# Six of eight attention-gate tiles in Strassen units ahead of attention, and a reordered start of the attention stage

## The reference

```
h = x + 0.5 * SwiGLU_1(RMSNorm(x))
u = RMSNorm(h)
[xp | q | k | v | gate_logits] = u @ w_in      # 512 | 512 | 512 | 512 | 2048 columns
y_pool = (causal multi-scale pooling of xp) @ w_branch_pool
y_sb   = (strictly causal stick-breaking attention, 8 heads of 64) @ w_branch_attn
m = sigmoid(g_pool) * y_pool + sigmoid(g_sb) * y_sb
h = h + m @ w_out
h = h + 0.5 * SwiGLU_2(RMSNorm(h))
out = RMSNorm_final(h)
```

## Time and profile before

| what | value |
|---|---|
| median of 3 runs | 1917.43 us (1917.35 to 1917.62) |
| the profiled execution, its own time | 1918.11 us |
| its span, first to last instruction | 1916.2 us |
| TensorE busy | 1903.5 us (99% of the span) |
| VectorE, ScalarE, GpSimd busy | 1372.2, 796.4, 115.9 us |
| granted TensorE clock, mean | 0.999 of full speed |
| mix stage, from its first to its last matmul | 707.7 to 821.9 us |
| attention stage | 909.3 to 1149.8 us |

### The profile page before, as it was taken

The page is one execution under the profiler, slowest core; times in us unless marked ns, Lnnn a source line. Parts: engine busy times, 40 slices in busy tenths (PEclk is TensorE's granted clock), DMA queues, the critical chain, the costliest instruction groups (busy, mean ns, idle before and its releaser), DMA issues.

```text
span 1916.2 us, 24977 instructions
## 1 busy us (share of the span) xinstructions
PE 1903.5 (99%) x9010; PEld 1592.0 (83%) x9010; DVE 1372.2 (72%) x1677; ACT 796.4 (42%) x1175; POOL 115.9 (6%) x157
## 2 busy tenths in 40 slices
PE   9999999999999999999999999999999999999998
PEld 8888888888888888888888888898888888888887
DVE  6978777784566776488677768889777777756555
ACT  7423232323434544234676752474323232324344
POOL 1000000000000300000233220010000000000001
PEclk9999999999999999999999999999999999999999
DMA  5456654558676733416875447643545444677665
GB/s 165 144 198 230 223 181 140 199 189 306 208 240 201 195 110 132 132 50 181 226 174 148 128 139 260 197 138 119 178 144 196 149 169 153 216 264 244 206 192 206
DMA packets 258419, 348.24 MB, mean 182 GB/s; under 512 B 29344, under 2 KB 161184, under 8 KB 255008
## 3 DMA queue, kind: packets, MB, share of 16 engines
q1 hardware_dynamic: 258336, 347.15, 56.3%
HBM read 233.83 MB, written 112.99 MB: 181 GB/s over the span
## 4 chain that ended last, share of the span: by engine, by line
PE 97%; DVE 1%; DMA 1%; issue 0%; SPq 0%; ACT 0%; POOL 0%; POOLq 0%; DVEq 0%; ACTq 0%
PE bank L1263 40%; PE bank L1372 9%; PE bank L1319 9%; PE bank L1321 9%; PE bank L1320 9%; PE bank L1513 6%; PE bank L1215 3%; PE bank L1449 2%; PE bank L1421 2%; PE bank L1479 2%; PE bank L1585 2%; PE bank L1604 1%; PE bank L1190 1%; PE bank L1603 1%; PE bank L1570 1%; PE bank L1568 1%
## 5 line engine op out<-in xcount | busy, mean ns | idle before, releaser
L2253 DVE TENSOR_TENSOR dn_lo<-dn_lo_raw,dn_hi 128x1024 fp32r<-128x1024 f32 x149 | 181.9, 1224 | 149.6 <-ACT dn_hi L1788 149.1
L1263 PE MATMUL bank<-lo_t,wa_hi 128*128 128x512 f32 x656 | 252.8, 389 | 0.0
L1263 PE MATMUL bank<-hi_t,wa_hi 128*128 128x512 f32 x656 | 252.8, 389 | 0.0
L1263 PE MATMUL bank<-hi_t,wa_lo 128*128 128x512 f32 x656 | 252.8, 389 | 0.0
L1788 ACT ACTIVATE dn_hi<-dn_lo_raw 128x1024 fp32r<-128x1024 f32 x149 | 158.0, 1061 | 218.8 <-DMA dn_lo_raw<-act_dram 218.8
L1319 PE MATMUL bank<-dn_hi 128*128 128x512 f32 x596 | 232.7, 390 | 0.0
L1321 PE MATMUL bank<-dn_lo,dn_hi 128*128 128x512 f32 x596 | 231.9, 389 | 0.0
L1320 PE MATMUL bank<-dn_hi,dn_lo 128*128 128x512 f32 x596 | 231.9, 389 | 0.0
L1263 PE MATMUL bank<-hi_b,wa_hi 128*128 128x512 f32 x492 | 190.6, 389 | 1.0 <-DVE up L2387 1.0
L1263 PE MATMUL bank<-lo_b,wa_hi 128*128 128x512 f32 x492 | 190.5, 389 | 0.0
L1263 PE MATMUL bank<-hi_b,wa_lo 128*128 128x512 f32 x492 | 190.4, 389 | 0.0
(11 more groups left out here) (275 smaller groups left out, 3747.7 us busy)
## 6 DMA issues: line engine op xcount, KB each, us to landing
wa_lo_raw<-in_ffn_w_gate_up_dram SPq DMA_DIRECT2D x87, 512.0 KB, 5.0
dn_lo_raw<-act_dram SPq DMA_DIRECT2D x149, 256.0 KB, 4.2
act_dram<-g SPq DMA_DIRECT2D x44, 512.0 KB, 4.4
wd_t<-in_ffn_w_down_dram SPq DMA_DIRECT2D x44, 512.0 KB, 6.6
act_dram<-s_of SPq DMA_DIRECT2D x88, 256.0 KB, 6.5
wd_dram<-wd_t SPq DMA_DIRECT2D x22, 1024.0 KB, 6.0
dn_lo_raw<-wd_dram SPq DMA_DIRECT2D x85, 256.0 KB, 3.4
dn_lo_raw<-in_ffn_w_down_dram SPq DMA_DIRECT2D x64, 256.0 KB, 3.0
```

Source lines behind the costliest of these rows:

```text
L1263: last = nc.tensor.matmul(acc, lhs, rhs, start=n == 0 and i != 2 and i < 5, stop=n == 11, skip_group_check=True)
L2253: return nc.vector.tensor_tensor(dst, raw, hi.bitcast(f32), ALU.subtract)
```

## The change

Six gate tiles of kind 1 go through the mix stage in place of four: `EARLY` becomes 6, the mix stage has 7 units, the attention stage 5 gate units (480 matmuls), three of them of kind 0 alone. Since the number of units is now odd, the second plain q, k unit computes in banks 4 to 7 and the bank halves of the mix units are `(b + NM + 1) % 2`; the branch weights after attention swap their two buffers. `pool_y` gets a place of its own, and SP loads the first head and two blocks of `pool_y` ahead of the weights of gate unit 1. The four split pieces of that unit come later (`piece_step`). `SHARE` stays as it is.

```diff
-EARLY = 4
+EARLY = 6
...
-    return gate_step(piece_start(j) + (7 + 18 * piece if j < NG - 1 else 1 + 6 * piece))
+    return gate_step(piece_start(j) + (26 if j == 1 else 7) + (16 if j == 1 else 18) * piece if j < NG - 1 else piece_start(j) + 1 + 6 * piece)
...
-        pool_y = at("pool_y", [P, 2, HALF], f32, G0)
+        pool_y = at("pool_y", [P, 2, HALF], f32, o + 16384)
...
             gate_unit(0)
             spill_pool_branch(2)
-            gate_unit(1)
...
             load_head(0)
+            sp_.wait_ge(y_even_sp, 16)
+            load_pool_y(0)
+            sp_.wait_ge(y_sp[1], 16)
+            load_pool_y(1)
+            gate_unit(1)
             spill_pool_branch(3)
             load_head(1)
             for b in range(4):
                 sp_.wait_ge(y_sp[b], 16 * (KT // 2 if b else KT // 4))
             sp_.wait_ge(y_even_sp, 16 * (KT // 4))
-            load_pool_y(0)
-            load_pool_y(1)
             gate_unit(2)
...
-                    wait_bank(b, q)
+                    if not fresh:
+                        pe.wait_ge(tr_free, 4 * NT)
...
-                        last = products(bank[:, b, :], par, ab, lambda kt: u_hi[:, kt, cols],
+                        last = products(bank[:, b if fresh else 4 + b, :], par, ab, lambda kt: u_hi[:, kt, cols],
...
-                s = (b + 1) % 2
+                s = (b + NM + 1) % 2
...
-                    if b == 0 and i == 0:
-                        pe.wait_ge(tr_free, 4 * NT)
-                    if b == 1 and i in (0, 1, 3, 4):
-                        wait_bank(place, Q_A[1] + 1)
+                    if b < 2 and i in (0, 1, 3, 4):
+                        wait_bank(place, Q_A[b] + 1)
...
-                branch_tile(j, j % 2, j // 2)
+                branch_tile(j, (U_C + j) % 2, j // 2)
```

More of the change, by code:

```diff
@@ L1945, in take_first @@
                 act.wait_ge(acc_ready, 4 * Q_A[m] + b + 1)
-                nc.scalar.activation(ring_hi[n % 3][:, th * HALF:(th + 1) * HALF], bank[:, b, :], ACT.Copy,
+                nc.scalar.activation(ring_hi[n % 3][:, th * HALF:(th + 1) * HALF], bank[:, 4 * m + b, :], ACT.Copy,
                                      scale=1.0 if ab else QSCALE).then_inc(ev_hi, 1)
@@ L1969, in mix_first @@
                 act.wait_ge(mb_prod, 7 * b + 1)
-                nc.scalar.activation(mix_dst(b, 0, 0), bank[:, 4 * ((b + 1) % 2), :], ACT.Copy).then_inc(mb_copied, 1)
+                nc.scalar.activation(mix_dst(b, 0, 0), bank[:, 4 * ((b + NM + 1) % 2), :], ACT.Copy).then_inc(mb_copied, 1)
             def mix_second(b):
@@ L1976, in mix_second @@
                     act.wait_ge(mb_add, 5 * b)
-                nc.scalar.activation(mid[:, :], bank[:, 4 * ((b + 1) % 2), :], ACT.Copy).then_inc(mb_copied, 1)
+                nc.scalar.activation(mid[:, :], bank[:, 4 * ((b + NM + 1) % 2), :], ACT.Copy).then_inc(mb_copied, 1)
             def mix_post(b, a, th, adds):
@@ L2221, in outputs_hi @@
                 nc.scalar.activation(o_piece(u_hi, i), o_piece(xu, i), ACT.Copy).then_inc(o_hi, 1)
-            act.wait_ge(raw_in[KT % 2], 32 * (U_C // 2 + 1))
+            act.wait_ge(raw_in[U_C % 2], 32 * (U_C // 2 + 1))
             act.wait_ge(gate_ready, GATE_LAST[NG - 2] + 1)
-            nc.scalar.activation(w_hi[:, KT % 2, 0, 0:BR], w_raw[:, KT % 2, 0, 0:BR], ACT.Copy).then_inc(whi, 1)
+            nc.scalar.activation(w_hi[:, U_C % 2, 0, 0:BR], w_raw[:, U_C % 2, 0, 0:BR], ACT.Copy).then_inc(whi, 1)
             for i in range(len(O_PARTS)):
@@ L2232, in split_branch @@
             def split_branch(j):
-                act.wait_ge(raw_in[j % 2], 32 * ((U_C + j) // 2 + 1))
+                act.wait_ge(raw_in[(U_C + j) % 2], 32 * ((U_C + j) // 2 + 1))
                 act.wait_ge(acc_ready, 4 * Q_C + 2 * (j - 1))
-                nc.scalar.activation(w_hi[:, j % 2, 0, 0:BR], w_raw[:, j % 2, 0, 0:BR], ACT.Copy).then_inc(whi, 1)
+                nc.scalar.activation(w_hi[:, (U_C + j) % 2, 0, 0:BR], w_raw[:, (U_C + j) % 2, 0, 0:BR], ACT.Copy).then_inc(whi, 1)
             for n in range(1, KT):
@@ L2690, in take_first @@
                 cols = slice(th * HALF, (th + 1) * HALF)
-                nc.vector.scalar_tensor_tensor(out=ring_lo[(2 * m + ab) % 3][:, cols], in0=bank[:, b, :], scalar=1.0 if ab else QSCALE,
+                nc.vector.scalar_tensor_tensor(out=ring_lo[(2 * m + ab) % 3][:, cols], in0=bank[:, 4 * m + b, :], scalar=1.0 if ab else QSCALE,
                                                in1=ring_hi[(2 * m + ab) % 3][:, cols].bitcast(f32), op0=ALU.mult,
@@ L2755, in mix_c11 @@
                 dst = mix_dst(b, 0, 0)
-                nc.vector.tensor_tensor(dst, bank[:, 4 * ((b + 1) % 2) + 1, :], dst, ALU.add).then_inc(mb_add, 1)
+                nc.vector.tensor_tensor(dst, bank[:, 4 * ((b + NM + 1) % 2) + 1, :], dst, ALU.add).then_inc(mb_add, 1)
             def mix_c22(b, part):
-                dst, s = mix_dst(b, 1, 1), (b + 1) % 2
+                dst, s = mix_dst(b, 1, 1), (b + NM + 1) % 2
                 if part:
@@ L2776, in mix_c12 @@
                 dve.wait_ge(mb_prod, 7 * b + 6)
-                nc.vector.tensor_tensor(mix_dst(b, 0, 1), bank[:, 4 * ((b + 1) % 2) + 2, :], mid[:, :], ALU.add).then_inc(mb_add, 1)
+                nc.vector.tensor_tensor(mix_dst(b, 0, 1), bank[:, 4 * ((b + NM + 1) % 2) + 2, :], mid[:, :], ALU.add).then_inc(mb_add, 1)
             def mix_c21(b):
                 dve.wait_ge(mb_prod, 7 * b + 7)
-                nc.vector.tensor_tensor(mix_dst(b, 1, 0), bank[:, 4 * ((b + 1) % 2) + 3, :], mid[:, :], ALU.add).then_inc(mb_add, 1)
+                nc.vector.tensor_tensor(mix_dst(b, 1, 0), bank[:, 4 * ((b + NM + 1) % 2) + 3, :], mid[:, :], ALU.add).then_inc(mb_add, 1)
             def mix_out(b, a, th, posts):
@@ L3084, in _ @@
                     dve.wait_ge(whi, U_C + 1)
-                    nc.vector.tensor_tensor(flat(w_lo[:, KT % 2, 0, 0:BR]), flat(w_raw[:, KT % 2, 0, 0:BR]),
-                                            flat(w_hi[:, KT % 2, 0, 0:BR]).bitcast(f32), ALU.subtract).then_inc(wlo, 1)
+                    nc.vector.tensor_tensor(flat(w_lo[:, U_C % 2, 0, 0:BR]), flat(w_raw[:, U_C % 2, 0, 0:BR]),
+                                            flat(w_hi[:, U_C % 2, 0, 0:BR]).bitcast(f32), ALU.subtract).then_inc(wlo, 1)
             outputs_lo(len(O_PARTS) - 1)
@@ L3119, in split_branch @@
                 dve.wait_ge(whi, U_C + j + 1)
-                dst, raw, hi = (flat(w[:, j % 2, 0, 0:BR]) for w in (w_lo, w_raw, w_hi))
+                dst, raw, hi = (flat(w[:, (U_C + j) % 2, 0, 0:BR]) for w in (w_lo, w_raw, w_hi))
                 nc.vector.tensor_tensor(dst, raw, hi.bitcast(f32), ALU.subtract).then_inc(wlo, 1)
```

## The result

| | before | after |
|---|---|---|
| median of the runs | 1917.5 us (1917.35 to 1917.62, 4 runs) | 1932.0 us (1930.48 to 1933.13, 4 runs) |
| ratio, 95% interval | | 1.0074 (1.0062 to 1.0086) |
| profiled execution: own time, span | 1918.1, 1916.2 us | 1931.8, 1929.8 us |

The change makes the kernel 14.5 us slower. The forecast was 1918.9, its range ended at 1923.0: wrong in size, and the slower case had been given 0.27. One run of the kernel before, beside the first experiments, took 6375 us at a granted clock of 0.29 and is left out of every comparison.

A forecast was written before the change was run, and what follows sets the result against it. TensorE, busy 1903.5 of 1916.2 us, was taken as the bound, provided gaps between matmuls stay covered. Terms -2.7 - 0.8 + 5.0 = +1.5 us on the profiled execution gave 1918.9 us against the median, range 1914 to 1923.

The forecast's parts named there:

- Part 1: Mix and attention stages: one more mix unit adds 19.0 us, the gate unit it replaces frees 21.8; net -2.7 us.
- Part 3: Attention chain: fewer gate matmuls to cover it open 5.6 us of TensorE gaps; +5.0 us net, bounds 1.5 to 10.
- Weighings: TensorE gaps before the weighings of blocks (7,6), (5,4) and (3,2): 1.4, 0.4 and 1.9 us.
- Reserve 0.05: Block 6's transposes to the weighing of (7,6): 0.05 us to spare, one filler fewer, two in one head; 1.4 us.
- Transposes of block 5: Interval from block 0's transposes to block 5's: two fillers go against 0.34 us of reserve; 1.9 us of gaps in all.
- The -0.6 of relief: ScalarE in attention: four gate evictions and four weight pieces leave, some of them in a chain; -0.6 us.
- The GpSimd rival: GpSimd's products stretch attention scans in five named steps, four hits taken: 3.9 us on top, 1922.8 us; chance 0.23.
- Part 2: Start of attention: first head's keys load ahead of gate unit 1's weights, wait 1.8 to 1.0 us; -0.8 us.
- the megabyte is most of what stands ahead of those loads: Start of attention: gate unit 1's 1 MB of weights mainly delays the k_lo loads; reason for taking a 1.0 us wait.
- the other bound: Start of attention: keys land at 914.4 as before the change, wait 2.4 us, a loss of 0.6.
- the first loads only change places: Start of attention: the later spill holds up tile 2, keys gain nothing; +1.5 to +3 us, 1921; chance 0.05.
- The chain keeps up: Attention chain: gaps may not add, as one lengthens the next interval's start; 1 us in all, 1914.9 us; chance 0.27.

The follow-up runs named there:

- thinned: Kernel before with every sixth gate matmul of the attention stage left out, banks, products and pieces unmoved: 1909.8 us.
- the small products: Changed kernel with GpSimd's gate products cut to 8 of their 512 columns: 1926.6 us.
- the old order: Changed kernel with SyncE's old queue at the start of attention, gate unit 1's weights ahead of the first head, pool_y loads behind the second head's: 1930.0 us.
- the new places alone, with full cover: Changed kernel with 96 of its 480 attention-stage gate matmuls done twice, giving 576 as before: 1939.5 us.

## Why the prediction was wrong

**Part 1 held.** The mix stage is 19.0 us longer, gapless; the net of the matmuls is -2.7 us. The moved banks, ring places and branch buffers cost nothing that shows.

**Part 3 named the right mechanism and mis-sized it: 5.0 us forecast, 10.4 measured** in the chain of the kernel before with thinned fillers (13.5 - 3.1), and 14.1 in the changed kernel, where the new places come on top. Every interval that it listed opened. The errors, term by term, in the changed kernel:
- *Weighings.* The three terms, 3.7 us, measured 6.7. "Reserve 0.05" for (7,6) was no reserve: the changed kernel's gaps there are mostly 0.26 to 0.28, a whole filler over the 0.05 that already stood. The sum also left out the second filler that one head loses (0.2 us), and 0.8 us of the first head's gap is the late spill.
- *Transposes of block 5.* 1.9 against 5.4. I let this chain begin at block 0's transposes and counted two fillers. ScalarE is busy without a break from 974.62 until block 0's `at_hi` at 978.19: the backlog begins with block 5's own logits, whose sigmoids, the value split and an eviction stand in that queue. From those logits to the transposes stand 12 or 13 fillers in place of 15 or 16, so three or four went, up to 0.9 us per head. Moving the split (1.06 us) closed most of the gap in two of the three heads that prepare values. In head 7 and in part in head 1 the gap is GpSimd's product.
- *Transposes of block 4* had no term; 1.7 us, 1.0 each in heads 0 and 5. These two vanish with the small products.
- *The -0.6 of relief* for fewer evictions and pieces on ScalarE doesn't show: at least, no gap shrank.

**The GpSimd rival was right, and wrongly set apart.** It was priced at 3.9 us on top; cutting the products gave back 5.4 us, 4.0 of it in the chain. That the price came out is partly luck. Of the five steps that it named, 12 and 60 were hit (978.46, the rows above; 1140.74, a product of 1.29 us ahead of a 1.20 us gap), 16, 30 and 38 were not; the other two costly hits were on block 4, which it had not named. The number of stretched scans is as before. They became dear for two reasons: their cover was gone (0.7 us of the chain in the kernel before, 2.0 thinned, in the same steps), and they fell in places with less reserve (4.0 in the changed kernel, with as few fillers as the thinned one). I had counted lost cover and collisions as two cases with chances of their own. They are not: what takes the cover lights every collision under it. So the range should have reached the sum, 1918.9 + 3.9 and the upper bound of 10 for Part 3: 1928. I wrote that bound down and then let the range end at 1923. Even 1928 is short of 1932.0. The Trainium skill ("SBUF — State Buffer", section "SBUF: two separate sides") has the two engines lock a shared port pair, so that the later one blocks until the first is done. By that the scan begun at 978.72 waits for the product's end at 979.74, 1.0 us; it was 0.9 longer than 1.75. The trace agrees.

**Part 2: the gain of 0.8 did not come.** The step that failed is "the megabyte is most of what stands ahead of those loads": with it or without it the keys arrive 2.9 to 4.1 us after their last issue, so it wasn't what held them, and what does is left open. The changed kernel met the other bound (a wait of 2.5 us for a forecast 2.4). And "I take nothing" for tile 2's sigmoids was wrong: the spill took 4.9 us to issue in place of 2.2, they waited 1.37, and the first weighing came 0.8 us later than with the old order. That rival (the first loads only change places) had 0.05; whether the whole order costs its 1.5 to 3 us is not shown.

**The chain keeps up** (0.27) is refuted. Its argument, that gaps in one interval lengthen the next one's start and so don't add, fails because each interval has its own chain: moving a filler changed its own interval.

**The account.** Between the two profiled executions lie 13.7 us: -2.7 (matmuls) + 14.1 (chain) + 0.7 (keys) + 1.1 (clock) + 0.5 (end of the stage). For the 14.1 there are two runs: thinning alone opened 10.4 in the chain, and the new places alone, with full cover, 3.1 (6.2 - 3.1). The 0.6 left may be the two together, or the way that the changed kernel deals its fillers out (12 or 13 in block 5's interval, the thinned one 12 to 14); no run separates them. The medians seem to say the same more simply, -2.7 + 13.8 (thinned) + 1.9 (order) = 13.0 of 14.5, but that sum is luck: 3.4 us of the 13.8 stand at the end of the stage, in the clock and in the keys' wait, and the 1.9 is mostly keys and clock.

## What to carry to other kernels

Work that fills the waits of another chain has two prices: its own time, and the waits that it hides. Measure the second before removing any of it, by leaving out the same share of fillers in the kernel at hand: here one such run would have said +13.8 us against a gain of 2.7. Then see in its trace where the time stands: two totals can agree and have different parts. Look for a chain's root in the queue of each engine in it, not only at the instruction that released its last link. And cases that one cause brings together don't get separate chances; their prices add in the range.

## What the runs showed of the hardware

After the 2.1 us stand-still ahead of 981.41 TensorE's granted clock fell. Windows of TensorE in the changed kernel (length, busy us, clock, DMA share, GB/s):

```profile
979.30:981.40 2.10, 0.23 (x3) 1.00 0.40 135
981.40:982.70 1.30, 1.29 (x9) 0.99 0.85 242
982.70:985.20 2.50, 2.50 (x8) 0.50 0.08 23
985.20:987.00 1.80, 1.80 (x11) 0.75 0.00 0
```

At 0.50, which is 1.2 GHz of 2.4, gate matmuls start 0.43 us apart in place of 0.2266; six intervals of that kind are 1.1 us, the line "slowed by the clock" in the table. The thinned kernel has the same at its start: after 2.0 us without a matmul, ahead of 914.05, the clock was 0.50 from 914.9 to 917.8. The length of the stand-still doesn't decide it in these traces: the run with the old order had the same gap as the changed kernel (2.09 us) and no fall, and the changed kernel itself stood for 2.5 us ahead of 933.21 and kept 1.00. Whether this explains the 2.7 us between the changed kernel's four runs was not tried; the kernel before, with 0.3 us over its first four runs, had 1.1 to 3.4 us over the later sets of 13 to 24. The Trainium skill ("TensorE: Matmul & The Clock Gate", section "What's actually happening") names these two clock levels and ties the lower one to idleness; the row agrees.
